# Where the split activations begin in SBUF, counted from a multiple of 1024 bytes

## The reference, cut to what matters

```
first_block : x += rms(mix(attention(q,k,v), rg_lru(...)) @ w_out);  up = conv(h @ w_up);  ffn = (gelu(g) * u) @ w_down
second_block, layer 0 : neighborhood attention (h @ w_qkv, softmax, @ w_o), then (silu(gate) * up) @ w_down, 2816 wide
second_block, layer 1 : mla (h @ w_down, @ w_uq, @ w_ukv, softmax, @ w_o), then 8 experts of 1792, top 2 per token
def _swiglu(h, w_gu, w_down):
    gate, up = jnp.split(h @ w_gu, 2, axis=-1)
    return (jax.nn.silu(gate) * up) @ w_down
```

## Time and profile before

| | us |
|---|---|
| median of 3 runs | 1264.17 |
| lowest and highest run | 1259.12, 1264.4 |
| span of the profiled execution | 1258.0 |
| PE busy in it | 1224.1 (97%) |
| DVE busy | 1016.2 (81%) |
| ACT busy | 779.0 (62%) |

### The profile page before, as it was taken

How to read it: one execution, slowest core, us unless ns; L and a number is a source line. 1 busy time by engine, 2 the same in 40 slices (tenths; PEclk the granted TensorE clock), 3 DMA queues, 4 the chain that set the end, 5 groups by cost and what they waited for, 6 DMA issues and landing times.

```text
span 1258.0 us, 20244 instructions
## 1 busy us (share of the span) xinstructions
PE 1224.1 (97%) x7668; PEld 1086.8 (86%) x7668; DVE 1016.2 (81%) x1095; ACT 779.0 (62%) x992; POOL 93.1 (7%) x111
## 2 busy tenths in 40 slices
PE   9989999999999999999999999999999999999995
PEld 7978999987998799998897777898989898989884
DVE  6797899996756588777756578989898989898987
ACT  5765666644655455443346556777777777777764
POOL 0020000000562100000002202000000000000020
PEclk9999999999999999999999999999999999999998
DMA  9953997679944569998973239999999999999991
GB/s 322 377 200 102 337 314 270 246 289 252 250 159 162 181 215 325 332 349 308 382 253 97 79 140 394 379 406 355 401 351 409 348 408 349 408 345 411 347 410 73
DMA packets 163981, 369.08 MB, mean 293 GB/s; under 512 B 24420, under 2 KB 96559, under 8 KB 157511
## 3 DMA queue, kind: packets, MB, share of 16 engines
q1 hardware_dynamic: 157345, 350.72, 78.0%
q10 hardware_dynamic: 5094, 12.11, 2.5%
q0 software_dynamic: 1472, 5.28, 1.1%
HBM read 360.72 MB, written 14.70 MB: 298 GB/s over the span
## 4 chain that ended last, share of the span: by engine, by line
PE 71%; DVE 12%; ACT 4%; issue 4%; DMA 3%; SPq 3%; POOL 2%; ACTq 0%; DVEq 0%
PE ps L1341 20%; PE ps L795 7%; PE ps L797 7%; PE ps L796 7%; PE ps L1368 6%; PE ps L807 4%; PE ps L809 4%; PE ps L811 4%; DVE wlo L1893 3%; SPq L712 2%; PE ps L859 2%; PE ps L867 2%; DMA raw<-in_moe_w_gu 2%; DVE third_lo L1893 2%; DVE wlo L1885 1%
## 5 line engine op out<-in xcount | busy, mean ns | idle before, releaser
L1406 ACT ACTIVATE whi<-raw 128x1024 fp32r<-128x1024 f32 x186 | 192.6, 1057 | 152.0 <-PE ps L797 96.1
L1885 DVE TENSOR_TENSOR wlo<-raw,whi 128x1024 fp32r<-128x1024 f32 x186 | 227.1, 1248 | 72.8 <-ACT whi L1406 69.3
L795 PE MATMUL ps<-ahi,whi 128*128 128x256 f32 x832 | 234.3, 282 | 0.3 <-ACT qT L1591 0.3
L796 PE MATMUL ps<-alo,whi 128*128 128x256 f32 x832 | 231.8, 279 | 0.0
L797 PE MATMUL ps<-ahi,wlo 128*128 128x256 f32 x832 | 231.8, 279 | 0.0
L1893 DVE TENSOR_TENSOR wlo<-raw,whi 128x1792 fp32r<-128x1792 f32 (+1 forms) x96 | 199.3, 2089 | 24.4 <-ACT whi L1420 24.3
L1420 ACT ACTIVATE whi<-raw 128x1792 fp32r<-128x1792 f32 (+1 forms) x96 | 167.5, 1758 | 55.9 <-PE ps L1368 24.0
L795 PEld LDWEIGHTS ps<-ahi,whi 128*128 128x128 f32 x832 | 156.9, 189 | 1.7 <-issue 0.8
L796 PEld LDWEIGHTS ps<-alo,whi 128*128 128x128 f32 x832 | 156.7, 188 | 0.7 <-issue 0.7
L797 PEld LDWEIGHTS ps<-ahi,wlo 128*128 128x128 f32 x832 | 156.9, 189 | 0.0
L1341 PE MATMUL ps<-whi,hchi 128*128 128x448 f32 x352 | 101.8, 370 | 4.0 <-DVE wlo L1893 2.7
(11 more groups left out here) (350 smaller groups left out, 2431.7 us busy)
## 6 DMA issues: line engine op xcount, KB each, us to landing
raw<-in_moe_w_gu SPq DMA_DIRECT2D x96, 896.0 KB, 7.0
ada<-in_w_ada SPq DMA_DIRECT2D x48, 1024.0 KB, 7.4
raw<-in_moe_w_down SPq DMA_DIRECT2D x32, 1024.0 KB, 7.9
ada<-in_moe_w_gu SPq DMA_DIRECT2D x32, 896.0 KB, 7.3
raw<-in_w_up SPq DMA_DIRECT2D x22, 1024.0 KB, 5.8
raw<-in_ffn_w_gu SPq DMA_DIRECT2D x22, 1024.0 KB, 9.1
ada<-in_moe_w_down SPq DMA_DIRECT2D x16, 1024.0 KB, 9.2
raw<-in_na_w_qkv SPq DMA_DIRECT2D x12, 1024.0 KB, 8.4
```

The costliest lines, as they stand in the source:

```text
L795: pe.matmul(o, h[:, k, cols], bhi[:, k], start=(k == 0), stop=False)
L796: pe.matmul(o, h[:, k, cols], blo[:, k], start=False, stop=False)
L1406: act.activation(high_, src, ACT.Copy).then_inc(hi_done, 1)
L1885: ve.tensor_tensor(low_, src, high_.bitcast(F32), ALU.subtract).then_inc(lo_done, 1)
```

## The change

`ahi` and `alo` begin 64 bytes lower, at the same offset from a multiple of 1024 bytes as `whi` and `wlo`. `third_hi` and `third_lo` keep their addresses, since the 64 bytes that were taken off `ahi_at` and `alo_at` for them are no longer taken off, and so does all that follows, since the padding grows by the same 64 bytes. `warm`, which lies on `alo`, moves with it.

```diff
@@ -335,7 +335,6 @@
         x = at("x", NT * D).rearrange("p (t n) -> p t n", t=NT)
         xn_at = room(NT * D)
         xn = at("xn", NT * D, offset=xn_at).rearrange("p (t n) -> p t n", t=NT)
-        room(HALF_LINE)
         ahi_at = room(KT * S)
         ahi_flat = at("ahi", KT * S, F32R, offset=ahi_at)
         alo_at = room(KT * S)
@@ -345,9 +344,9 @@
         hx = at("hx", NT * D, offset=xn_at).rearrange("p (t k s) -> p t k s", t=NT, k=KT)
 
         raws = [raw[:, s] for s in range(NRAW)] + [ada[:, s] for s in range(NADA)]
-        whi = [whi2[:, s] for s in range(NSPLIT)] + [at("third_hi", CHUNK, F32R, offset=ahi_at - HALF_LINE * 4)]
-        wlo = [wlo2[:, s] for s in range(NSPLIT)] + [at("third_lo", CHUNK, F32R, offset=alo_at - HALF_LINE * 4)]
-        room(ROUND - HALF_LINE)
+        whi = [whi2[:, s] for s in range(NSPLIT)] + [at("third_hi", CHUNK, F32R, offset=ahi_at)]
+        wlo = [wlo2[:, s] for s in range(NSPLIT)] + [at("third_lo", CHUNK, F32R, offset=alo_at)]
+        room(ROUND)
         gates_at = room(2 * D)
         gates = at("gates", 2 * D, offset=gates_at).rearrange("p (g n) -> p g n", g=2)
         gvec = at("gvec", D)
```

## The result

The changed kernel takes 1268.49 us, the median of 12 runs (1267.09 to 1271.64); the kernel before, run beside it, 1264.12 (12 runs, 1258.21 to 1265.83). The ratio on record is 1.0062, with a 95% interval of 1.0047 to 1.0076. It is no plain quotient: the medians lie 4.4 us apart, which is a ratio of 1.0035, and the means 1.0047. The kernel is slower by all three, and the size is 0.35 to 0.6%. The time lies inside the forecast range of 1252 to 1277, but on the side that got a chance of 0.33; the forecast was no change.

The account below looks back on a forecast made before the run. The prediction took PE to bound the kernel nearly everywhere, so only the pace of matmuls counted. From the median 1264.2 it took 0.8 us for the output projections and zero for the 256-column matmuls: 1263.4 us, range 1252 to 1277.

Parts of the forecast that it names:

- the side that got a chance of 0.33: Whole kernel: the outcome that the changed kernel is measurably slower, chance 0.33.
- Step 1, what moves: `ahi` and `alo` move to the offset of `whi`; `ghi`, `third_hi` and everything behind stay; no cost, no gain.
- What bounds the kernel: PE nearly everywhere, gapless in both up-projection streams of 960 matmuls; a nanosecond per matmul there is a microsecond.
- The run shown and the median: Both long up-projection streams slow in the median run, only the first in the profiled one; 4.2 us per stream.
- Step 2, output projections: 512-column matmuls, stationary from `ahi`/`alo`: 6.5 ns faster each, 120 on the chain, 0.8 us off, bounds 0.8 and 1.3.
- Step 3, value chunks: 256-column matmuls with `ahi` as stationary, lines 807, 809, 811: nothing taken, bounds -1.3 and +1.3 us.
- Step 4, the 256-column matmuls of `columns_form`: `ahi` as moving operand, lines 795 to 797, 2496 matmuls: zero taken; bounds 4.4 ns down, some 4.5 up each.
- rival B: Equal starts always fall into step, both long streams at 113.3 ns: 10.5 us faster, 1253.7 us; chance 0.25.
- C: Equal starts make the gapless reads of `columns_form` meet every time: 4.5 ns more each, 11.2 us, 1274.6 us; chance 0.35.
- its point of decision: 256-column matmuls with `ahi` as moving operand: the slower outcome decides from 2.8 ns per matmul on.
- A: Offsets don't matter, or the streams keep their habits: 1263.4 us, 1264.2 without the output projections' gain; chance 0.40.

Follow-up runs that it names:

- `shift_320`: Kernel before with the split activations 320 bytes past the offset of the split weights instead of 64: 1258.54 us in its one run.
- `shift_192`: Kernel before with the split activations 192 bytes past the offset of the split weights instead of 64: 1263.34 us, ratio 1.0033.
- part 2 alone: Kernel before with only output projections 2 and 3 written and read through views at equal offsets, all else at 64 bytes: 1259.78 us, ratio 1.0009.
- the bursts: Separate kernels of split matmuls alone, other engines at rest, one operand offset after another: 113.3 to 122.3 ns from start to start at 256 columns.
- `shift_112_outputs_equal`: Kernel before with split activations 112 bytes past the split weights' offset, output projections 2 and 3 at equal offsets through views: 1257.52 us, ratio 0.9982.
- `shift_256`: Kernel before with the split activations 256 bytes past the offset of the split weights instead of 64: 1268.78 us, ratio 1.0067.
- `columns_equal`: Changed kernel, but output projections 2 and 3 written and read through views 64 bytes higher, as in the kernel before: 1270.20 us, ratio 1.0072.

## Why the prediction went wrong

**Step 1, what moves:** right. The `ghi` rows are unchanged, the experts' part differs by no more than between two traces of the kernel before, and in `shift_320` `ahi` was moved by 256 bytes and both paces stayed.

**What bounds the kernel:** right. PE has no gap in either stream, before or after, and 1 ns per matmul was 1 us per stream: 2.2 and 6.7 ns gave 2.1 and 6.4 us.

**The run shown and the median:** half right. "One stream at the other pace is 960 x 4.4 ns = 4.2 us" holds in size (4.3 in `shift_192`). The 1.1 us around the span were wrong: they came from two different executions, and wherever one execution has both figures it is 1.8 or 1.9 (1267.09 against 1265.3 after). By that the execution shown took some 1259.8, an estimate, and the median lies 4.3 above it, again one stream. That both streams of the median run are slow was not seen in any trace of the kernel before.

**Step 2, output projections:** right in sign and in the price of a pair (453 against 467 ns), a little large in sum. 0.8 us was taken; the ledger gives 0.5 in the changed kernel and 0.6 with part 2 alone. A few uneven starts at the beginning of a sequence take a part back: in the third output projection of after, the single starts from 720 on are 231, 236, 228, 233, 231 ns apart, and 226 to 227 only then.

**Step 3, value chunks:** the sign was not known, zero was taken. Their mean length rose from 278 to 283, and the median distance of their starts is 120 ns after, 113 or 118 before. Against both paces that is at most 288 x 6.7 ns = 1.9 us, a little outside the bound of 1.3; what of it reaches the end can't be told from what varies between 300 and 430.

**Step 4, the 256-column matmuls of `columns_form`:** this is the step that failed. It took zero for each, and measured are 2.2 ns more than the slow pace and 6.7 more than the fast one. The zero came from one matmul at each of two changes of form, read as "an equal start neither helped nor harmed". A single pass at distance 0 does start on time; before it and after it stand passes at 64, and it is the sequence of passes at one distance that has a pace. The text itself held rows against it: uneven starts of the first pairs at distance 0, and PEld gapless in the 256-column streams, so that nothing is left over in which to fall into step. (Its "half its length free" for 512 columns does not follow from its own 0.19 of 0.227, and between 569.7 and 577.4 PEld is busy 6.38 of 7.70 us; free is a sixth.) The rows of the 512-column matmuls pulled towards rival B, and the measured order for them is the opposite of the order for 256 columns: 226.7 against 233.3, but 120.0 against 113.3 or 117.8. The nearest row by shape was no row of a stream. No row of before shows a stream of this shape at the new distance, so zero was a guess in the middle, and the text gave it the largest chance.

**The rivals.** C had the direction and the place: both gapless streams are slower at equal offsets, and the sign that would show it ("about 820 starts in 100 us") came out as 836. Whether the two reads meet, as C says, no run can show; that the loss hangs on the distance of the two operands alone, the bursts do. Its size was wrong: 4.5 ns on top of the slow pace was put, twice the 2.2 found, because it came from the shaking pairs of another shape. The 2.8 ns of its point of decision stood against a median with both streams slow; against the two traces the mean of 2.2 and 6.7 is some 4.4 ns, and there it is passed. B fell whole, and `shift_112_outputs_equal` (1257.5) shows that its 1253.7 was wrong even with fast streams and its part 2: DVE does not let the first stream run at 113.3 to its end, and the DVE share of the earlier trace rows, 106.73 of 114, had been called "barely" enough. A fell since the old paces were not seen at distance 0: none in 20 bursts of 20 at 0, 256 and 512, and none in six long streams of six (after, `shift_256`, `columns_equal`).

The Trainium skill's rule that PE's two reads are independent (SBUF - State Buffer, "Who interferes with whom") was weighed and refused on the 512-column rows. The bursts confirm this: with all other engines at rest, the distance of the two operands alone moves a 256-column matmul from 113.3 to 120.0 ns.

## What to carry to other kernels

Where PE is gapless with a weight load for every matmul of 256 columns, the distance between moving and stationary operands modulo 256 bytes was worth 6.7 ns of each matmul between the best distance (113.3) and equal offsets (120.0). Equal offsets were among the worst for 256 columns (only 72 and 120 bytes were slower), and the best of four for 512, so the choice goes by the shape that holds the time, and data of both shapes can be read through two views. A distance that has one pace (112 here) is surer than one that has two and whose start decides (64, 192), though here DVE left only 1.1 of the 4.3 us that a fast first stream could give, and the kernel at 112 was no faster in the median (ratio 1.0001). Work out first whether another engine keeps up with the faster stream, and count starts per 100 us in a gapless stretch to see which pace a stream has. A single instruction at a new relation is no row for a stream of them.

## What the runs showed of the hardware that was not expected

- A 256-column fp32r matmul with its own weight load has three even paces, 113.3, 117.8 and 120.0 ns, at one clock (1.00), and at other distances uneven ones with means up to 122.3; which are open to it depends on the distance modulo 256 bytes (256 and 512 like 0, 320 like 64; 128 like neither).
- At a distance of 64 or 192 the stream keeps whichever of two paces it came into: 20 bursts at 64 and 320 split 16 to 4, 20 at 192 and 448 split 6 to 14 (slow to fast), and the first stream of the kernel was slow from its start in five traces of six. In the sixth it was fast until a late start and slow after it.
- 64 bytes in one operand's place cost a kernel of 1264 us 4.4 us between the medians, without an instruction, wait or transfer being changed.
